# Second norm's transposes moved from TensorE to DMA in a transformer layer on eight cores

## The reference, cut to what matters

```python
def layer_norm(x, g=None, b=None):
    mu = mean(x); var = mean((x - mu) ** 2)
    y = (x - mu) * rsqrt(var + 1e-5)
    return y if g is None else y * g + b

merged = sigmoid(ga) * (ya @ w_a) + sigmoid(gb) * (yb @ w_b)       # token mixer, last part
x_mid  = layer_norm(ALPHA * x + mod[2] * (merged @ w_out), ln1_g, ln1_b)
h2     = layer_norm(x_mid) * (1 + mod[4]) + mod[3]                  # the second norm, scale and shift
gate, up = split(h2 @ w_ffn_in)                                     # 1024 -> 2 x 2816
x_new  = layer_norm(ALPHA * x_mid + mod[5] * ((silu(gate) * up) @ w_ffn_out), ln2_g, ln2_b)
```

## Time and profile before

| | |
|---|---|
| time, median of 3 runs | 987.92 us (987.78 to 989.19) |
| the profiled execution | 987.81 us |
| its span, slowest core (core 6) | 986.3 us |
| spans of the eight cores | 978.2 to 986.3 us |
| busy: PE, DVE, ACT, POOL | 901.2, 471.0, 297.2, 243.4 us |
| DMA queues: from POOL (software), from SP (hardware) | 40.44 MB, 54.06 MB |

### The profile page before, as it was taken

One profiled execution on the slowest core, in us unless ns is written; L12 is line 12 of the kernel. 1 busy time (PEld: TensorE's weight loads), 2 busy tenths in 40 slices (PEclk: granted clock), 3 DMA queues, 4 the chain that ended last, 5 costly groups with the idle time before them and its releaser, 6 DMA issues.

```text
span 986.3 us, 15419 instructions; the slowest of 8 cores (978.2 to 986.3 us)
## 1 busy us (share of the span) xinstructions
PE 901.2 (91%) x5401; PEld 434.9 (44%) x5401; DVE 471.0 (48%) x930; ACT 297.2 (30%) x408; POOL 243.4 (25%) x282
## 2 busy tenths in 40 slices
PE   0569998899999999999989999999999999999993
PEld 0324444445444444444444444444444444444443
DVE  2146665376632456656666321121122114777775
ACT  1215555599922232433333311111111111000000
POOL 5023333256532345555543003010000000000000
PEclk9989999999999999999999999999999999999997
DMA  9988876069720022217713039972211004233231
GB/s 169 169 190 204 175 177 95 3 118 178 137 108 1 1 87 85 73 57 164 157 65 86 22 53 158 167 114 43 35 16 36 1 1 150 92 122 113 101 107 45
DMA packets 41069, 95.50 MB, mean 97 GB/s; under 512 B 4000, under 2 KB 4512, under 8 KB 40992
## 3 DMA queue, kind: packets, MB, share of 16 engines
q0 software_dynamic: 21136, 40.44, 26.6%
q1 hardware_dynamic: 19856, 54.06, 16.9%
HBM read 118.14 MB, written 16.78 MB: 137 GB/s over the span
## 4 chain that ended last, share of the span: by engine, by line
PE 77%; DMA 9%; ACT 5%; DVE 3%; issue 3%; POOL 1%; another core or an unknown queue 0%; SPq 0%; DVEq 0%; ACTq 0%; POOLq 0%
PE bank L1088 30%; PE bank L953 16%; PE bank L1223 14%; DMA arena<-wada 7%; PE bank L984 5%; ACT arena L812 3%; PE bank L488 2%; DMA arena<-xh 2%; PE bank L809 1%; PE bank L558 1%; PE bank L805 1%; PE bank L528 1%; PE bank L828 1%; ACT arena L428 1%; PE bank L1041 1%
## 5 line engine op out<-in xcount | busy, mean ns | idle before, releaser
L1088 PE MATMUL bank<-arena 128*128 128x512 bf16 x1408 | 305.4, 379 | 0.0
L1088 PEld LDWEIGHTS bank<-arena 128*128 128x128 bf16 x1408 | 137.6, 98 | 165.4
L953 PE MATMUL bank<-arena 128*128 128x512 bf16 x768 | 168.0, 379 | 0.0
L1099 DVE TENSOR_TENSOR arena<-bank,arena 128x512 bf16<-128x512 f32 x88 | 60.9, 692 | 224.2 <-PE bank L1088 217.2
L1223 PE MATMUL bank<-arena 128*128 128x512 bf16 (+1 forms) x748 | 152.2, 366 | 0.0
L1097 ACT ACTIVATE arena<-bank 128x512 f32<-128x512 f32 x88 | 52.4, 595 | 224.9 <-PE bank L1088 224.9
L953 PEld LDWEIGHTS bank<-arena 128*128 128x128 bf16 x768 | 75.0, 98 | 89.9
L1223 PEld LDWEIGHTS bank<-arena 128*128 128x128 bf16 x748 | 73.2, 98 | 79.1
L969 DVE TENSOR_TENSOR arena<-bank,arena 128x512 f32<-128x512 f32 x64 | 44.3, 692 | 94.0 <-PE bank L953 94.0
L812 ACT ACTIVATE arena<-bank 128x1024 bf16<-128x1024 f32 x80 | 76.3, 1027 | 4.8 <-PE bank L809 4.5
L962 ACT ACTIVATE arena<-bank 128x512 f32<-128x512 f32 x64 | 37.0, 591 | 118.9 <-PE bank L953 118.9
(11 more groups left out here) (110 smaller groups left out, 867.2 us busy)
## 6 DMA issues: line engine op xcount, KB each, us to landing
arena<-xh SPq DMA_DIRECT2D x34, 512.0 KB, 6.9
arena<-wada POOLq DMA_DIRECT2D x12, 1024.0 KB, 16.9
arena<-wff POOLq DMA_DIRECT2D x11, 1024.0 KB, 10.4
xmid_d<-arena SPq DMA_DIRECT2D x16, 512.0 KB, 2.9
arena<-xmid_d SPq DMA_DIRECT2D x16, 512.0 KB, 3.7
out<-arena SPq DMA_DIRECT2D x32, 256.0 KB, 2.0
arena<-wff POOLq DMA_DIRECT2D x11, 512.0 KB, 20.6
arena<-wout SPq DMA_DIRECT2D x16, 256.0 KB, 5.4
```

The source lines that it names most:

```text
L953: t_mm = S.op('pe', lambda e, k=k, n=n, p=bk(bank), lhs=w[:, lo + k, :], rhs=src[:, k, tok]: e.matmul(p, lhsT=lhs, rhs=rhs, start=(k == 0) ...
L1088: rhs=h2T[:, k, tok]: e.matmul(p, lhsT=lhs, rhs=rhs, start=(k == 0), stop=(k == 7)),
L1099: fb_free[b0 + 1] = sg_free[s_] = t_act[(f, tg)] = S.op('dve', lambda e, f=f, p=bk(b0 + 1), sg=sgb[s_]: e.tensor_tensor(out=act[f][:, tok] ...
```

## The change

`c2_turn` now takes one token tile: a DMA issued from SP reads the tile's 128x1024 bf16 from `xnb[t % 4]` and writes it turned into the 8 chunks of `h2T` (128 partitions x 8 x 128). It is put behind `c2_norm2` of the tile and waits for it. `c2_out` now takes a whole group: 8 VectorE instructions scale and shift 128x512 bf16 in place in SBUF; the first waits for the turns of all four tiles. It stands two units behind the group's last turn. TensorE's 128 transposes, ACT's 16 and DVE's 16 moves out of PSUM are gone, and `xnb[t % 4]` is free again when the tile's DMA has landed.

```diff
-    def c2_turn(g, half):
-        for i in range(4):
-            for n in range(4):
-                t_tr = S.op('pe', lambda e, i=i, c=half * 4 + n, dst=tp_view(6 + n // 2, n % 2)[:, i * 128:(i + 1) * 128]: e.transpose(
-                    dst, xnb[i][:, c * 128:(c + 1) * 128], ident),
-                    deps=[fb_free[6], fb_free[7], c2[4 * g + i]['n2']] if n == 0 else (), sig=(n == 3))
-            if half == 1:
-                xnb_free[i] = t_tr
-        c2[4 * g][('tr', half)] = t_tr
-
-    def c2_out(g, half):
...
-            if n < 2:
-                t_e = S.op('act', lambda e, dst=h2T[:, c, cols], src=tp_view(6, n), c=c: e.activation(
-                    out=dst, in_=src, func=AF.Identity, scale=mcol(3, c, 0), bias=mcol(2, c, 0)),
-                    deps=[c2[4 * g][('tr', half)], t_modc])
-            else:
-                t_e = S.op('dve', lambda e, dst=h2T[:, c, cols], src=tp_view(7, n - 2), c=c: e.tensor_scalar(
-                    out=dst, in0=src, scalar1=mcol(3, c, 0), scalar2=mcol(2, c, 0), op0=ALU.mult, op1=ALU.add),
-                    deps=[c2[4 * g][('tr', half)], t_modc])
-            fb_free[6 + n // 2] = t_e
-            t_h2[g].append(t_e)
+    def c2_turn(t):
+        c2[t]['tr'] = xnb_free[t % 4] = S.dma('sp', lambda e, src=xnb[t % 4], t=t: e.dma_start_transpose(
+            out=h2T[:, :, t * 128:(t + 1) * 128], in_=src), 'turn%d' % (t % 4), deps=[c2[t]['n2']])
+
+    def c2_out(g):
+        for c in range(8):
+            t_h2[g].append(S.op('dve', lambda e, h=h2T[:, c, g * 512:(g + 1) * 512], c=c: e.tensor_scalar(
+                out=h, in0=h, scalar1=mcol(3, c, 0), scalar2=mcol(2, c, 0), op0=ALU.mult, op1=ALU.add),
+                deps=[[c2[4 * g + i]['tr'] for i in range(4)], t_modc]))
...
+        at((u + 3, 'end') if t < 12 else (u + 4, 'end'), c2_turn, t)
         if t % 4 == 3:
-            g = t // 4
-            u2, gap = (u + 4, 1) if g < 3 else (u + 6, 2)
-            at((u2, 'mm'), c2_turn, g, 0)
-            at((u2 + 1, 'late'), c2_out, g, 0)
-            at((u2 + gap, 'mm'), c2_turn, g, 1)
-            at((u2 + gap + 1, 'late'), c2_out, g, 1)
+            at((u + 5, 'end') if t < 12 else (u + 6, 'end'), c2_out, t // 4)
```

More of the change, by code:

```diff
@@ L1036, in c2_norm2 @@
         wk_free[t % NWK] = [c2[t]['n2'], t_spill[t]]
-    def c2_turn(g, half):
-        for i in range(4):
-            for n in range(4):
-                t_tr = S.op('pe', lambda e, i=i, c=half * 4 + n, dst=tp_view(6 + n // 2, n % 2)[:, i * 128:(i + 1) * 128]: e.transpose(
-                    dst, xnb[i][:, c * 128:(c + 1) * 128], ident),
-                    deps=[fb_free[6], fb_free[7], c2[4 * g + i]['n2']] if n == 0 else (), sig=(n == 3))
-            if half == 1:
-                xnb_free[i] = t_tr
-        c2[4 * g][('tr', half)] = t_tr
-    def c2_out(g, half):
-        cols = slice(g * 512, (g + 1) * 512)
-        for n in range(4):
-            c = half * 4 + n
-            if n < 2:
-                t_e = S.op('act', lambda e, dst=h2T[:, c, cols], src=tp_view(6, n), c=c: e.activation(
-                    out=dst, in_=src, func=AF.Identity, scale=mcol(3, c, 0), bias=mcol(2, c, 0)),
-                    deps=[c2[4 * g][('tr', half)], t_modc])
-            else:
-                t_e = S.op('dve', lambda e, dst=h2T[:, c, cols], src=tp_view(7, n - 2), c=c: e.tensor_scalar(
-                    out=dst, in0=src, scalar1=mcol(3, c, 0), scalar2=mcol(2, c, 0), op0=ALU.mult, op1=ALU.add),
-                    deps=[c2[4 * g][('tr', half)], t_modc])
-            fb_free[6 + n // 2] = t_e
-            t_h2[g].append(t_e)
+    def c2_turn(t):
[6 more added lines that the diff above has]
+                deps=[[c2[4 * g + i]['tr'] for i in range(4)], t_modc]))
     w_free = [None] * NWR
```

## The result

| | before | after |
|---|---|---|
| time, median of 4 runs each | 988.56 us (987.78 to 989.79) | 982.54 us (982.02 to 986.05) |
| ratio, with its 95% interval | 1 | 0.9946 (0.992 to 0.9972) |
| the profiled execution, its span | 987.81, 986.3 us | 986.05, 984.4 us (core 2) |
| spans of the eight cores | 978.2 to 986.3 us | 975.5 to 984.4 us |

The change is faster, by 6.0 us in the medians. The forecast was 11.5 us: the sign was right, and half of the gain is missing; 982.54 lies just above the range's upper end of 982.5. Measured again beside the later experiments (e8), the same kernel gave 981.05 against 985.7 us (ratio 0.996, 0.9945 to 0.9975).

What follows compares the result with a forecast made beforehand. TensorE's list plus its stalls bound the kernel. Removing 7.1 + 0.9 + 3.0 + 1.7 = 12.7 us, less a 1.2 us stall, gave 11.5 us off 987.8: 976.3 us, range 974.5 to 982.5.

Steps and rivals of the forecast that it cites:

- Steps 1 and 2: TensorE loses 8 transpose batches, 7.1 us, and the waits before second halves in groups 0 and 1, 0.9 us.
- Step 4: After group 2's wait, TensorE's transposes and output projection ran below full clock; 1.7 us would come back.
- In groups 0, 1 and 3 ... cost nothing: In these groups DVE idles around each 3.5 us burst and TensorE has a bank pair in hand: no cost.
- The stall behind group 2's burst: TensorE waits 1.2 us for tile 14's projection banks, wanted at 523.4 but free at 524.6, ahead of tile 15's projection.
- third rival: ACT, DVE and POOL bound the kernel around group 2, so only 7.1 + 0.9 us go: 979.9 us; chance 0.13.
- The turns: The 16 turning DMAs on SP's list land in 2 to 6 us, within every group's slack, delaying nothing TensorE needs.
- 18 us of slack: In groups 0 and 1 a turn may take up to about 18 us from issue to landing without cost.
- first rival: Turns land late, 8.6 to 17 us, stalling group 2 and then group 3: 977 to 987 us; chance 0.12.
- The second: Turns land so late, past 17.3 us, that TensorE loses more than it wins: 997 us at 20; chance 0.10.
- Squares in series: If a tile's 8 squares went by DMA in series, a turn would take 10.5 us and the time be about 978.2.

Runs made afterwards that it cites:

- e8: The changed kernel again with no edit, measured beside later experiments: 981.05 us, ratio to before 0.996.
- e1: The changed kernel with all 32 in-place scale-and-shift instructions on DVE left out, turns kept: 974.84 us, ratio to before 0.9901.
- e3: The changed kernel with each burst of 8 cut into two of 4, ahead of a unit's product and behind L1015: 974.19 to 975.67 us, ratio to before 0.9903.
- e4: The kernel before with only TensorE's 128 transposes left out, the moves out of PSUM kept: 973.99 us, ratio to before 0.9892.
- e6: The changed kernel with bursts halved and placed behind L1015, and tiles 12 to 15 three units apart instead of two: 971.69 us, ratio to before 0.9864.
- e9: The changed kernel with whole bursts of 8 moved behind L1015 and ahead of a unit's product: 975.51 and 976.54 us, ratio to before 0.9905.
- e2: The changed kernel with the 16 turning DMAs left out, in-place instructions kept: 979.48 us, ratio to before 0.9951.

## Why the prediction was right and wrong

**Steps 1 and 2, transposes and the small waits: right.** C1 has four of the eight batches and both small waits. By the prediction these are 4 x 0.89 + 0.9 = 4.5 us; C1 goes from 212.0 to 207.2 wherever no burst disturbs it (e1, e3, e4, e6, e9), 4.8 us. Behind C1 the prediction had 8.2 us; gate/up goes from mostly 329.5 to 321.2 in e6, 8.3 us.

**Step 4, the low clock: right, for this core.** The granted clock is 1.00 in every window from 480 to 560 us of the change, against 0.93 and 0.98 before, although TensorE still idles for up to 2.86 us of a 20 us window there; the output projections take 3.61 us where one took 4.75. So the 1.7 us came back. That they were 1.7 is core 6's case: before, all eight cores idle 2.96 us at this place, and behind it core 3 kept its full clock (1.05 us for the transposes, 3.62 for the projection, gate/up 327.9), while core 2 paid 3 us (1.87 and 5.76, gate/up 330.8).

**The failed step: "In groups 0, 1 and 3 ... cost nothing".** For group 3 that held: TensorE's last stall ends at 546.71, ahead of its burst at 554.47. The bursts of groups 0 and 1, priced at nothing, cost C1 1.7 us (e8's 208.9 against e1's 207.2) and TensorE another 1.50 us behind it, at tile 12's projection. The prediction looked for the cover of each burst in DVE's idle time and TensorE's free banks. DVE's idle time was there. What it left out is what stands behind the burst in DVE's list: L1015, 0.2 us long, for which ACT (L1017) and through it POOL (L1024) wait, and for POOL waits DVE's L1028. DVE of the change around group 0's burst:

```profile
401.49 1.23 DVE L1028 TENSOR_TENSOR arena<-arena 128x1024 f32<-128x1024 f32 x1
...
410.07 3.62 DVE L1044 TENSOR_SCALAR arena<-arena 128x512 bf16<-128x512 bf16 x8
413.62 0.21 DVE L1015 SCALAR_TENSOR_TENSOR arena<-arena 128x1 f32<-128x1 f32 x2
...
418.84 2.20 DVE L1028 TENSOR_TENSOR arena<-arena 128x1024 f32<-128x1024 f32 x1 [0.67 <-POOL arena L1024]
```

L1015 goes out 3.6 us late, and L1028 comes 3.5 us late: 17.35 us from 401.49 to 418.84, where TensorE takes 13.81 for a tile. The idle times of ACT and POOL take up none of that, because each of them works once for a tile, in turn. In the new place (e3) the half burst stands behind L1015 and fills the very time in which DVE waits for POOL:

```profile
401.03 0.22 DVE L1015 SCALAR_TENSOR_TENSOR arena<-arena 128x1 f32<-128x1 f32 x2
401.17 2.34 DVE L1044 TENSOR_SCALAR arena<-arena 128x512 bf16<-128x512 bf16 x4
...
406.25 1.23 DVE L1028 TENSOR_TENSOR arena<-arena 128x1024 f32<-128x1024 f32 x1
```

**The delay stays.** The next tiles take 13.24 us (418.84, 432.08, 445.32): they gain only 0.57 us each on TensorE. Where L1028 keeps its 1.2 us, as in e9, a chain that is late takes 12.25 us (409.98 to 422.23, core 2) and has caught up after a tile. What makes the difference is a second effect. L1028 and POOL's L971 collide, and who comes second pays. Before, DVE came first:

```profile
398.64 1.23 DVE L1028 TENSOR_TENSOR arena<-arena 128x1024 f32<-128x1024 f32 x1
398.83 2.17 POOL L971 TENSOR_TENSOR arena<-arena 128x512 bf16<-128x512 f32 x1 [0.29 <-DVE arena L969]
```

After, POOL did:

```profile
458.79 1.26 POOL L971 TENSOR_TENSOR arena<-arena 128x512 bf16<-128x512 f32 x1
458.93 2.21 DVE L1028 TENSOR_TENSOR arena<-arena 128x1024 f32<-128x1024 f32 x1 [0.67 <-POOL arena L1024]
```

So L1028, which lies in the chain, takes 1 us longer in six tiles running, and its mean over the kernel shows it:

```profile
L1028 DVE TENSOR_TENSOR arena<-arena 128x1024 f32<-128x1024 f32 x16 | 25.4, 1591 | 4.3 <-POOL arena L1024 4.0
```

It was 1222 ns before and is 1224 in e3. Group 1's burst then comes upon a chain that has not caught up, and TensorE stops three times (0.55, 0.86, 1.50 us). One burst is covered, the second isn't: a look at one burst at a time, as the prediction's, can't see this. How much is due to the late L1015 and how much to the longer L1028, no run parts: where the burst stands behind L1015 (e3, e9), L1028 keeps its length in all tiles but one of e9. The Trainium skill, "SBUF — State Buffer", "SBUF: two separate sides", says that DVE and GpSimd share one pair of ports by an exclusive lock and that the second to start is blocked until the first ends; the rows agree: L1028 starts 1.12 us ahead of L971's end and takes 0.98 us longer.

**The stall behind group 2's burst (1.2 us forecast): right as one stall, too small as the sum, because a rate was missed.** Ahead of tile 15's projection TensorE waited 1.00 us; but 1.89, 0.64 and 0.44 us come behind it, 2.97 us that the prediction did not have. It followed tile 14 alone. In the gate/up phase the chain from one tile's L1028 to the next tile's takes 11.2 us:

```profile
508.81 1.23 DVE L1028 TENSOR_TENSOR arena<-arena 128x1024 f32<-128x1024 f32 x1
...
518.65 3.65 DVE L1044 TENSOR_SCALAR arena<-arena 128x512 bf16<-128x512 bf16 x8
...
522.28 1.21 DVE L1028 TENSOR_TENSOR arena<-arena 128x1024 f32<-128x1024 f32 x1
...
533.46 1.23 DVE L1028 TENSOR_TENSOR arena<-arena 128x1024 f32<-128x1024 f32 x1
...
544.63 1.23 DVE L1028 TENSOR_TENSOR arena<-arena 128x1024 f32<-128x1024 f32 x1
```

From 522.28 on the steps are 11.18 and 11.17 us; e1, without bursts, has the same (510.05, 521.22, 532.39, core 5), and e3 too. TensorE, with the transposes gone, needs 3 x 3.45 = 10.4 us for two units and a projection. It gains 0.8 us a tile on the chain and stops when the banks in hand are used up. And over group 2's burst the step is 13.47 us, 2.3 more. In the kernel before the three steps from 506.99 to 542.65 took 35.66 us; in the change, from 508.81, 35.82. TensorE's list became shorter there, the chain's did not. That is the third rival's mechanism (0.13), though spread over units 38 to 43 and with the low clock's 1.7 us won all the same. What it costs by itself is small: 1.6 us of stalls in e1 and e3. The bursts' part is larger, gate/up 327.3 against 323.4, 3.9 us.

**The sum, as it turned out.** The prediction had 12.7 off and 1.2 on. Measured from before to e6: 13.2 off with every cover in place. From there on: 2.2 us for two units' spacing (e3 against e6), where the prediction had nothing, and 5.7 for the bursts, whole and in their place (e1 against e8's 536.2), where it had 1.2. 13.2 - 2.2 - 5.7 = 5.3 us, which is 541.5 less e8's 536.2 again. The first ratio gives 5.3 us too (0.0054 x 988.56), e8's ratio 3.9 (0.004 x 985.7).

**The turns: right, with one place tight.** They land in 2.8 us, and behind them on SP nothing was late that TensorE waited for: without them (e2) the stalls are the same. In group 1, beside w1's loads, the longest on each core of the first trace took 10.2 to 15.3 us, more than the forecast's 6, and it was nearer than the prediction's 18 us of slack. Core 4 of the change:

```profile
448.12 2.04 SPq L1039 DMA_TRANSPOSE arena<-arena  x1
...
463.75 2.67 DVE L1044 TENSOR_SCALAR arena<-arena 128x512 bf16<-128x512 bf16 x8 [3.86 <-DMA arena<-arena]
...
469.59 8.79 PE L953 MATMUL bank<-arena 128*128 128x512 bf16 x39 [3.45 <-ACT arena L962]
```

This turn landed 15.3 us after its issue, DVE waited 3.86 us for it and TensorE then idled 3.45 us in place of core 2's 0.55; C1 takes 211.6 us there instead of 208.7. Of the 18 us of slack, DVE was there after 11.8 us (12.7 forecast), and of the 5.2 us of banks behind that only 1 was left (3.86 waited, 2.9 lost). That fits a chain which group 0's burst had made late already, since the other cores stall at this place with no late turn. The late turns are the first rival's mechanism, on one core. The second (slower, from 17.3 us on in all groups) was not met.

**Squares in series.** The Trainium skill, "VectorE: DVE Perf Modes", "The three transpose paths", gives 1309 ns for one 128x128 by DMA; eight in series would be, as an estimate from it, 10.5 us. The rows don't bear out the series: a tile of eight landed in 2.8 us, 0.35 us a square.

## What to carry to other kernels

When a change takes work from the bounding engine, write down the period of every ring of engines that feeds it (here DVE, ACT, POOL, DVE: 11.2 us a tile) beside that engine's new period (10.4): where the ring is the slower, its pace is the one you get. Price a block of added instructions by what stands behind it in its engine's list, not by the engine's idle time: the same 32 instructions cost 5.7 us ahead of a 0.2 us scalar that two other engines wait for, 1.5 behind it, and nothing behind it in halves. A delay goes away only if the chain runs clearly faster than the engine it feeds, so look at two bursts in succession and not at one.

## What the hardware did that was not expected

- The turn of 256 KB from SBUF to SBUF lands in 2.8 us, like SP's plain spills (2.9), but its issue holds SP for 1.24 us. It makes 1,056 packets for a tile. The longest landing was 15.3 us, beside the weight loads.
- A DVE instruction with two inputs and a POOL instruction in SBUF slow each other by order of start: 1.23 against 2.20 us for L1028, 1.27 against 2.17 us for L971. Which of the two pays is set by microseconds of timing far ahead, and then stays for six tiles.
- The same idle time of 2.96 us cost the eight cores between nothing and 3 us of lower clock, and one of 1.83 us ahead of C1 cost 0.9 to 1.4 us on some cores and nothing on others; 1.89 us in gate/up cost no core any.
- The in-place scale and shift of 128x512 bf16 took 0.40 us; the Trainium skill, "VectorE: DVE Perf Modes", "The perf-mode tier table", led to an estimate of 0.3 us. The measured 0.40 decides, for this instruction with its two scalars for each partition; it is nearer to half of the 0.69 us of the earlier trace rows than to the 0.53 from PSUM.
